# Two recurrent decoder layers on one core: other places for gating, decode steps, modulation pieces and the reload of x

## The reference

```python
mod = silu(c) @ ada_w + ada_b
shift, scale, gate = split(mod, 3)
h = rms_norm(x, norm_g) * (1 + scale) + shift
proj = h @ w_in                 # columns of four branches A, B, C, D and of the merge gates
oA = rwkv7_branch(...)          # chunked for the prompt, one state step for the samples
oB = retention_branch(...)
oC = rglru_branch(...)
oD = gdn_branch(...)            # gated delta rule
merged = sum over n of sigmoid(gl[n]) * (branch[n] @ w_up[n])
x = x + gate * (merged @ w_out)
```

## Time and profile before

| what | value |
|---|---|
| median of 3 runs | 1532.18 us (1531.87 to 1536.23) |
| profiled execution | 1531.77 us |
| its span, first to last instruction | 1530.0 us |
| granted TensorE clock, mean | 0.972 |
| busy: PE, PEld | 1417.8 us (93%), 1283.5 us (84%) |
| busy: DVE, ACT, POOL | 641.9, 517.6, 473.3 us |
| DMA | 162.18 MB, mean 106 GB/s |

### The profile page before, as it was taken

How to read it: one execution, slowest core, us unless ns; L and a number is a source line. 1 busy time by engine, 2 the same in 40 slices (tenths; PEclk the granted TensorE clock), 3 DMA queues, 4 the chain that set the end, 5 groups by cost and what they waited for, 6 DMA issues and landing times.

```text
span 1530.0 us, 33517 instructions
## 1 busy us (share of the span) xinstructions
PE 1417.8 (93%) x14880; PEld 1283.5 (84%) x14880; DVE 641.9 (42%) x1115; ACT 517.6 (34%) x780; POOL 473.3 (31%) x350
## 2 busy tenths in 40 slices
PE   6799999999999999897979999999899999989896
PEld 4698999989899888775879898999888988878695
DVE  5756412417322336535133861132444242663522
ACT  5533422224422244143433252221542223514322
POOL 0244522123312122157723452122322122312620
PEclk9899999999999999998999999999999999999998
DMA  9532231225321354476543323122263126246811
GB/s 318 181 97 70 73 91 45 58 57 110 109 76 51 64 107 121 102 261 212 166 127 83 94 70 84 44 51 63 70 142 83 44 57 120 76 121 174 272 42 56
DMA packets 275908, 162.18 MB, mean 106 GB/s; under 512 B 86102, under 2 KB 244922, under 8 KB 275252
## 3 DMA queue, kind: packets, MB, share of 16 engines
q1 hardware_dynamic: 274100, 159.06, 38.1%
q10 hardware_dynamic: 1664, 0.98, 0.2%
HBM read 135.25 MB, written 24.89 MB: 105 GB/s over the span
## 4 chain that ended last, share of the span: by engine, by line
PE 75%; DVE 13%; ACT 5%; issue 3%; DMA 2%; ACTq 1%; SPq 1%; POOL 0%; DVEq 0%
PE psA L836 31%; PE psA L844 15%; PE psA L886 6%; PE psB L772 3%; PE psB L781 3%; PE psB L782 2%; PE psB L717 2%; DVE RA L1946 1%; PE psB L959 1%; DVE small_rows L1837 1%; DMA RB<-in_ada_w 1%; PE psB L969 1%; PE psB L1402 1%; ACT w_hi L1436 1%; DVE small_rows L1838 1%
## 5 line engine op out<-in xcount | busy, mean ns | idle before, releaser
L708 POOL TENSOR_TENSOR w_lo<-ring,w_hi 128x512 fp32r<-128x512 f32 x274 | 381.7, 1415 | 941.7 <-ACT w_hi L1436 881.0
L836 PE MATMUL psA<-h_hi,w_hi 128*128 128x260 f32 x1984 | 428.9, 298 | 23.2 <-DVE h_lo L1852 12.8
L836 PE MATMUL psA<-h_lo,w_hi 128*128 128x260 f32 x1984 | 404.2, 286 | 0.0
L836 PEld LDWEIGHTS psA<-h_hi,w_hi 128*128 128x128 f32 x1984 | 310.5, 191 | 41.8 <-issue 19.9
L836 PEld LDWEIGHTS psA<-h_lo,w_hi 128*128 128x128 f32 x1984 | 310.8, 191 | 0.2
L844 PE MATMUL psA<-h_hi,w_lo 128*128 128x260 f32 x1984 | 274.5, 286 | 0.0
L844 PEld LDWEIGHTS psA<-h_hi,w_lo 128*128 128x128 f32 x1984 | 249.6, 187 | 5.3 <-issue 1.0
L1436 ACT CAST w_hi<-ring 128x1024 fp32r<-128x1024 f32 x133 | 137.2, 1033 | 32.4 <-PE psA L844 18.8
L787 ACT COPY ws<-psB 128x128 f32<-128x128 f32 x80 | 21.4, 268 | 248.6 <-PE psB L772 248.6
L795 DVE COPY_PREDICATED tg<-tmask,psB 128x128 f32<-128x128 uint8 x40 | 14.2, 356 | 133.4 <-PE psB L782 95.2
L1466 ACT ACTIVATE tg<-psA 128x520 f32<-128x520 f32 x48 | 28.8, 600 | 88.5 <-PE psA L844 88.3
(11 more groups left out here) (476 smaller groups left out, 2356.7 us busy)
## 6 DMA issues: line engine op xcount, KB each, us to landing
ring<-in_w_in SPq DMA_DIRECT2D x122, 512.0 KB, 4.2
scr_tanh<-tg SPq DMA_DIRECT2D x48, 260.0 KB, 4.6
ring<-in_ada_w SPq DMA_DIRECT2D x18, 512.0 KB, 4.4
upw<-in_w_up SPq DMA_DIRECT2D x64, 128.0 KB, 3.9
RA<-scr_tanh SPq DMA_DIRECT2D x30, 260.0 KB, 4.1
RB<-in_ada_w SPq DMA_DIRECT2D x14, 512.0 KB, 5.7
ws<-scr_tanh SPq DMA_DIRECT2D x24, 260.0 KB, 4.4
ring<-in_w_out SPq DMA_DIRECT2D x9, 512.0 KB, 4.9
```

Of the source, the lines that this page charges most:

```text
L708: nc.gpsimd.tensor_tensor(tile_part(RL[s][:, k], (kind, n)), tile_part(RS[s][:, k], (kind, n)), tile_part(HS[L.hslot[q]][:, k], (kind, n)) ...
L836: nc.tensor.matmul(out(h), HS[L.hslot[q]][:, p, 0:m], cols(part(p), h), start=(p == 0 and part is hi), stop=False)
```

## The change

Retention: the gating of branch C goes from the pause of c = 0 to that of c = 1, the decode step from c = 1 to c = 2, and SP writes its results after `up` 15 in place of `gate` 28. Tails: in layer 0 ups 20 and 22 have no piece any more, so that 12 pieces stand beside ups and 12 beside outs 0 to 5; in layer 1 the eight pieces move from ups 18 to 25 to ups 24 to 31, and `mods(1)` behind out 0. The reloads of x move from ups 19, 22, 25 and 28 to up 30 and outs 0, 1 and 3. The first square sum is taken together with the second. Half decode passes: each part of `decode_a` and `decode_d` is done in two halves (8 of 16 rows or columns per partition), one in group 1, one in group 2. The tables of semaphore steps follow and are left out here, as are the remaining parts of the two decode functions, which change in the same way.

```diff
-                tail = [x for k in range(18, 32) for x in [("up", k)] + [("ada", k - 18)] * (k - 18 < self.n_ada)]
-                tail += [x for k in range(KT) for x in [("out", k)] + [("ada", m) for m in (14 + 2 * k, 15 + 2 * k) if m < self.n_ada]]
+                with_piece = [k for k in range(18, 32) if k not in (20, 22)] if n == 0 else list(range(24, 32))
+                self.up_piece = {k: m for m, k in enumerate(with_piece)}
+                self.out_pieces = [[m for m in (12 + 2 * k, 13 + 2 * k) if m < self.n_ada] for k in range(KT)]
+                tail = [x for k in range(18, 32) for x in [("up", k)] + [("ada", self.up_piece[k]) for _ in range(k in self.up_piece)]]
+                tail += [x for k in range(KT) for x in [("out", k)] + [("ada", m) for m in self.out_pieces[k]]]
...
-                    if x == ("gate", 28):
+                    if x == ("up", 15):
                         decode_results(2)
...
-                    if kind == "up" and n in (19, 22, 25, 28):
-                        m = (n - 19) // 3
+                    if x in (("up", 30), ("out", 0), ("out", 1), ("out", 3)):
+                        m = (("up", 30), ("out", 0), ("out", 1), ("out", 3)).index(x)
                         sp.wait_ge(*pm.at("gl", 31))
                         sp.dma_start(xT[:, 2 * m:2 * m + 2, :], scrX[:, 2 * m:2 * m + 2, :]).then_inc(L.xin[m], 16)
...
                 for idx in range(18, 32):
                     up(idx)
-                    if idx - 18 < n_ada:
-                        ada(idx - 18)
-                if layer:
-                    mods(1)
+                    if idx in L.up_piece:
+                        ada(L.up_piece[idx])
...
-                    for n in (14 + 2 * e, 15 + 2 * e):
-                        if n < n_ada:
-                            ada(n)
+                    for n in L.out_pieces[e]:
+                        ada(n)
+                    if layer and e == 0:
+                        mods(1)
...
-                    if e:
+                    if e == 2:
+                        square_sums(0)
+                    if e >= 2:
                         square_sums(e - 1)
...
                 for i in range(14):
-                    if i < n_ada:
-                        mod_rows(i)
+                    if 18 + i in L.up_piece:
+                        mod_rows(L.up_piece[18 + i])
                     if i >= 7:
                         m_hi(i - 7)
                 m_hi(KT - 1)
                 for e in range(KT):
                     split_ahead("out", e)
-                    for n in (14 + 2 * e, 15 + 2 * e):
-                        if n < n_ada:
-                            mod_rows(n)
+                    for n in L.out_pieces[e]:
+                        mod_rows(n)
...
-                def decode_a(part):
+                def decode_a(part, e):
-                    S0, tmp = wfC[:, 0:1024], wfC[:, 1024:2048]
-                    r_, w_, k_, a_, b_ = (vecA[:, n, :] for n in (0, 1, 2, 4, 5))
+                    rows = slice(8 * e, 8 * e + 8)
+                    S0, tmp = vk(wfC[:, 0:1024])[:, rows], vk(wfC[:, 1024:2048])[:, rows]
+                    r_, w_, k_, a_, b_ = (bc(vecA[:, n, :], 1, 8) for n in (0, 1, 2, 4, 5))
                     if part == 0:
-                        decode_in(0)
-                        did(ds, "1", T_(vk(tmp), vk(S0), row(a_), mult))
+                        if e == 0:
+                            decode_in(0)
+                        did(ds, "1", T_(tmp, S0, a_, mult), e)
...
-                    if j == 2:
-                        decode_a(5)
-                        decode_a(6)
+                    if j in (1, 2):
+                        decode_a(5, j - 1)
+                        decode_a(6, j - 1)
...
-                def decode_d(part):
+                def decode_d(part, e):
+                    cols = slice(8 * e, 8 * e + 8)
...
                         did(dc, "keep", v.tensor_copy(hkeep[:], RC[:, 0:2, SEQ - 1:TT]))
+                    elif c == 1:
                         dve.wait_ge(*an.at("tz", 2))
                         gated(2, RC[:, 0:2, :], RC[:, 2:4, :])
-                    elif c == 1:
+                    elif c == 2:
                         decode_in(2)

```

More of the change, by code:

```diff
@@ L1987, in _ @@
                 did(da, "prep", T_(q4(RA[:, 0:2, :]), psB[:, :, 0:HALF], q4(RA[:, 4:6, :]), mult))
-                def decode_a(part):
-                    S0, tmp = wfC[:, 0:1024], wfC[:, 1024:2048]
-                    r_, w_, k_, a_, b_ = (vecA[:, n, :] for n in (0, 1, 2, 4, 5))
+                def decode_a(part, e):
+                    rows = slice(8 * e, 8 * e + 8)
+                    S0, tmp = vk(wfC[:, 0:1024])[:, rows], vk(wfC[:, 1024:2048])[:, rows]
+                    r_, w_, k_, a_, b_ = (bc(vecA[:, n, :], 1, 8) for n in (0, 1, 2, 4, 5))
                     if part == 0:
-                        decode_in(0)
-                        did(ds, "1", T_(vk(tmp), vk(S0), row(a_), mult))
+                        if e == 0:
+                            decode_in(0)
+                        did(ds, "1", T_(tmp, S0, a_, mult), e)
                     elif part == 1:
-                        v.tensor_reduce(sa[:, 0, :], vk(tmp), AX.X, add)
-                        did(ds, "2", T_(vk(S0), vk(S0), row(w_), mult))
+                        v.tensor_reduce(sa[:, 0, rows], tmp, AX.X, add)
+                        did(ds, "2", T_(S0, S0, w_, mult), e)
                     elif part == 2:
-                        did(ds, "3", T_(vk(tmp), bc(sa[:, 0, :], 2, HD), row(b_), mult))
+                        did(ds, "3", T_(tmp, bc(sa[:, 0, rows], 2, HD), b_, mult), e)
                     elif part == 3:
-                        did(ds, "4", T_(S0, S0, tmp, add))
+                        did(ds, "4", T_(S0, S0, tmp, add), e)
                     elif part == 4:
-                        did(ds, "5", T_(vk(tmp), bc(vv[:, 0, :], 2, HD), row(k_), mult))
+                        did(ds, "5", T_(tmp, bc(vv[:, 0, rows], 2, HD), k_, mult), e)
                     elif part == 5:
-                        did(ds, "6", T_(S0, S0, tmp, add))
+                        did(ds, "6", T_(S0, S0, tmp, add), e)
                     else:
-                        did(ds, "7", T_(vk(tmp), vk(S0), row(r_), mult))
-                        v.tensor_reduce(so[:, 0, :], vk(tmp), AX.X, add).then_inc(*ds.step("so"))
+                        did(ds, "7", T_(tmp, S0, r_, mult), e)
+                        last = v.tensor_reduce(so[:, 0, rows], tmp, AX.X, add)
+                        if e:
+                            last.then_inc(*ds.step("so"))
                 Ma = Mst[0]
@@ L2045, in _ @@
                         u_a(c0)
-                    if j == 2:
-                        decode_a(1)
+                    if j in (1, 2):
+                        decode_a(1, j - 1)
                     if j:
@@ L2161, in decode_d @@
                     elif part == 4:
-                        did(ds, "17", T_(S0, S0, tmp, add))
+                        did(ds, "17", T_(S0, S0, tmp, add), e)
                     elif part == 5:
-                        did(ds, "18", T_(kv(tmp), kv(S0), col(vecB[:, 3, :]), mult))
+                        did(ds, "18", T_(tmp, S0, col8(vecB[:, 3, :]), mult), e)
                     else:
-                        v.tensor_reduce(so[:, 1, :], kvT(tmp), AX.X, add).then_inc(*ds.step("so"))
+                        last = v.tensor_reduce(so[:, 1, cols], tmpT, AX.X, add)
```

68 lines of the change are left out of this document (35 added, 33 removed).

## The result

The changed kernel takes 1515.93 us (median of 4 runs, 1510.59 to 1518.89) against 1532.62 for the kernel before beside it: a ratio of 0.9883, 95% interval 0.9849 to 0.9916, or 18 us less. In six more runs it was 0.9887 (0.9861 to 0.9912). The forecast was 1508.1 with a range of 1496 to 1521: the side and the range hold; the time is 7.8 too low, the gain (23.7 forecast) 6 us short. The profiled execution is the slowest of the four, 1518.89 with a span of 1517.1.

A forecast was written before the change was run, and what follows sets the result against it. The prediction took TensorE's order of work plus some twenty stalls as the bound. Retention 7.6, half passes 4.2 and tails 11.9 sum to 23.7 us off the profiled 1531.77: 1508.1, range 1496 to 1521.

The forecast's parts named there:

- Retention: Retention loops of both layers: gating and decode one pause later shorten TensorE's waits, 7.6 us in all.
- Tails: Up 18 to out 0's end: moved pieces and reloads save 8.9 us in layer 0, 3.0 in layer 1.
- clock term: Retention, second chunk: the 3.83 us wait cost 1.6 us more per layer at lower clock; its shorter successor would not.
- the 0.3 a layer charged for the decode result: Retention, row transposes: a charge for the decode result's row read arriving late, bounds nothing or 2 us.
- the shorter one nothing: Retention: the wait of 1.57 us cost no clock behind it, and one of 1.28 should cost none.
- Half passes: Tree phases: halved decode passes over groups 1 and 2 remove TensorE's waits, 4.2 us in both layers.
- the 0.1 that I had left: Delta tree's end: of the 1.30 us wait, 0.1 us stays after halving the decode passes.
- The 1.5 that I took off each layer: Tails, out 0: TensorE waits about 2 us there; halved clock costs nothing to 3 us, 1.5 taken per layer.
- 7.4 + L: Tails: us from up 24 + j's start to the merge of up 26 + j's end; L, a load's landing, 5.5.
- the 7.1: Retention: us from the decode's end until TensorE needs its row read, against 4.5 plus a landing.
- Rival (a): Tails stay DMA-bound, loads landing in 7.5 us: 2 x 5 us less gain, 1518.1; chance 0.20.
- Rival (c): Decode rows arrive 2 to 3 us late a layer, half passes return half: 1514 to 1516; chance 0.07.

The follow-up runs named there:

- e1: The changed kernel run again with no edit: 1516.63 us, ratio 0.9887 to the kernel before.
- e2: The kernel before with only the retention edit (gating and decode step one pause later): ratio 0.9947 to the kernel before.
- e5: The changed kernel with whole decode passes again, retention and tails as changed: 1517.2 us, ratio 0.9899 to the kernel before.
- e4: The kernel before with only the tails edit (pieces moved, x reloaded later, first square sum deferred): ratio 0.9928 to the kernel before.
- e3: The kernel before with only the halved decode passes: ratio 0.9993 (0.9975 to 1.0012) to the kernel before.
- e12: The changed kernel with copies before extra work, merged_hi before splits, out 0's low parts last, bare ups 18 and 22, last merged_hi before last split: 1501.28 us.
- e8: The changed kernel with VectorE's copies of the next chunk ahead of a pause's scan, gating and decode: 1512.78 us in its profiled execution.

## Why the prediction was right in its steps and 6 us short in its sum

**Retention: right, with its clock term misplaced.** Gating's 2.55 left the pause (waits 1.44 and 1.17, forecast 1.28), the second chunk kept its clock, the wait of 1.57 moved to the fourth chunk (1.54, 1.55), and the row transposes waited for nothing: the 0.3 a layer charged for the decode result was 0. What failed is "the shorter one nothing": from the fourth wait's end to the row transposes TensorE took 7.24 and 7.29 us, against 5.62 without a wait in the trace of before:

```profile
645.01 0.43 PE L1337 MATMUL psB<-ws,M 64*64 64x128 f32 x4
...
650.63 0.29 PE L1093 MATMUL psB<-cst,small_rows 8*128 8x8 f32 x2
```

So 1.6 us were lost behind a wait that had cost nothing one chunk earlier. Over all profiles the place counts more than the length: a wait of 1.54 or 1.55 ahead of the fourth chunk cost it 11 times of 14 (not in one layer each of e1, e2 and e5), one of 1.54 to 1.57 ahead of the third, in the old order, once of 8 (e4). Why is open. Nor is the second chunk's clock safe: in layer 0 of e1 a wait of 1.66 there was followed by 7.14 in place of 5.62. In its own stages the part is worth 5.5 to 7.5, not a fixed 7.6.

**Half passes: the waits right, the worth wrong.** Both waits vanished, also the 0.1 that I had left: 4.7 against 4.2. In the whole time 1 to 2 of it show, with an error of about 3 (e3, e5). With the half passes the rest is 684.5 in the mean of nine profiles, without them 681.2 in five; but eight of the nine and only two of the five have the retention edit, which has the loss of 1.6 told above. Some 1.5 of the difference repeats with the half passes: the stages from 519.0 to 600.0 and from 1263.4 to 1343.6 take 81.4 to 81.7 each with them (one exception of eighteen, 80.2) and 80.1 to 81.1 without. In layer 0 the lower clock comes behind a wait of 2.25 for a tanh. In the trace of before it slows the first matmuls there:

```profile
563.02 2.10 PE L1294 MATMUL psA<-ws,gw 128*128 128x260 f32 x4 [2.26 <-ACT tg L1466]
564.56 1.00 PE L836 MATMUL psA<-h_hi,w_hi 128*128 128x260 f32 x2
```

In the changed kernel it falls later, and a second wait of 0.39 for ScalarE comes up:

```profile
565.89 1.14 PE L1296 MATMUL psA<-ws,gw 128*128 128x260 f32 x4 [2.25 <-ACT tg L1469]
567.42 0.80 PE L838 MATMUL psA<-h_hi,w_hi 128*128 128x260 f32 x2 [0.39 <-ACT ws L1739]
```

That is 0.4 us. In layer 1 the trace of before has a granted clock of 1.00 through the stage and the changed kernel 0.98, which is 1.4 us. That much is shown. What remains lies within the spread of the rest, and why the clock is lower in more of these runs is open.

**Tails: right in the mechanism, partly lucky in the size.** Up 24 at 16.9 and 12.2 after up 18 (16.4 and 11.6). Last subtraction done 32.1 and 32.6 after up 24 (32.1). Out 0's end 34.6 and 35.2 after it (34.5). Landings of layer 0's pieces 4.7 and 5.4 by tile (5.5). The stages gained 10.1 and 3.0, forecast 8.9 and 3.0. The 1.5 that I took off each layer for a clock halved inside out 0 was not paid, the granted clock is 1.00 in both stretches; without that charge layer 0's forecast is 10.4 and right. In layer 1 the way from up 18 to the end of the row sum took 1.4 longer than the schedule instead, so that two errors cancel there and the equal 3.0 is luck. A subtraction beside GpSimd took 1.34 to 1.77, median 1.37 and 1.55 by layer, against 1.3. The Trainium skill, SBUF — State Buffer, section "Who interferes with whom", which would have made it 2.06, was too high here, and by e12 it can be far too low.

**The sum.** The edited stages gave 23.3 where the terms say 23.7, so no term is mis-sized by more than 2.1 in its own stages. The step that failed is what the sum is taken off: "the profiled execution's 1531.77", one execution, with every stage that isn't edited taken to repeat. The runs of before have a median of 1534.15 (23 runs), so 2.4 was this execution's luck; on that base the forecast is 1510.5. Of the 5.5 to 6 that remain, 2 to 3 are the half passes', by the best figures of e3 and e5. The rest isn't settled: the fourth wait's clock takes 2.1 from the retention's term in the first profile, and the stage behind 813.2 another 1.6, yet the retention alone measured 8.1 by the whole time (e2), its interval 5.5 to 10.7. Two small sums of the prediction don't come out, and neither moves the forecast by more than 0.5: the parts of 7.4 + L add up to 7.3 + L, and 4.5 plus a landing of 3.9 is 1.3 above the 7.1, not 2. Rival (a), tails bound by DMA, names 1518.1, near the profiled time, by a mechanism that isn't there: landings were short, and the tails gave more than their term. Rival (c), 1514 to 1516, has the half passes give back half, about what e3 and e5 measured, but its late decode rows didn't show.

## What to carry to other kernels

Cost a removed wait by two prices, its length and what the clock loses behind it: the first repeats well here (a tree phase to 0.05 us), the second differs from execution to execution and was 0 or 1.6 us for the same 1.55, more often 1.6 in one place and 0 in another. Before you subtract from a profiled time, profile the kernel twice and see what stages repeat; here the stages that nobody had edited took 11 us of 680 more, nearly half of the edited stages' gain. When a stage gets shorter, look at what the next one's loads had used that time for (e8), and prefer an order that lets an engine do the awaited work first to one that only moves the extra work: these orders, with two more places, took the mean of the runs from 1515.8 to 1499.9 (e12).

## What the runs showed of the hardware

One subtraction of VectorE with two SBUF inputs, 0.69 us alone, took 8.33 us while GpSimd ran on end: it began at 680.95, GpSimd had six subtractions of 1.25 from 681.27 to 688.73, and it was done 0.55 us behind the last of them, and the next subtraction, with GpSimd idle, took 0.69 (e12). So it can stand through a whole run of GpSimd instructions and not only through one. But it needn't: in the changed kernel the same instruction took 1.34 to 1.77, also amid four GpSimd subtractions back to back, as the one at 699.44 above did in 1.67. GpSimd then:

```profile
696.35 5.90 POOL L710 TENSOR_TENSOR rb_lo<-RB,w_hi 128x512 fp32r<-128x512 f32 x4
```

These four took 5.90 us, where four took 5.01 in e12 with the subtraction standing: here both engines lost a little, there VectorE alone waited. What decides between the two isn't shown. The section of the Trainium skill named above (SBUF — State Buffer, "Who interferes with whom") lets the later of the two wait for a whole instruction of the other. As an estimate by it, with the durations of this trace, that is 0.69 + 1.25 = 1.94; the measurement differs, and decides.

The granted clock behind a wait isn't a function of the wait's length: with 0.95 us at 407 the 26 us around it had a granted clock of 0.93 and 0.87 in two executions of the kernel before and 0.74 in the changed one, the waits equal to 0.01 us. The 23 runs of one unchanged kernel spread over 13 us, and those with the lowest mean clock, 0.965 and 0.966, are the slowest, 1538 to 1542.
